# Expert routing rewritten as one selection pass with one place code, rounded-type counting matmuls, and a first expert pair that starts on its own gathered rows

## The reference, cut to what matters

```python
def hier_moe(h, w_group, b_group, w_expert, b_expert, w_gate, w_up, w_down):
    xt = h.reshape(-1, D); N = xt.shape[0]                       # 512 tokens
    g_prob = softmax(xt @ w_group + b_group)                      # 4 groups
    g_p, g_idx = lax.top_k(g_prob, 1)
    e_logits = (xt @ w_expert + b_expert).reshape(N, 4, 8)[the chosen group]
    e_p, e_idx = lax.top_k(softmax(e_logits), 2)
    w = g_p * e_p / sum(e_p)
    eid = g_idx * 8 + e_idx                                       # 2 of 32 experts per token
    # the rows of each expert are gathered into blocks, and each block does
    ys = (silu(xb @ w_gate[e]) * (xb @ w_up[e])) @ w_down[e]      # 1024 -> 256 -> 1024
    # out[token] = sum over its two experts of w * ys
```

## Time and profile before

| | us |
|---|---|
| median of 3 runs (1796.85 to 1800.13) | 1796.89 |
| the profiled execution | 1796.5 |
| its span in the profile | 1795.2 |
| TensorE busy | 1650.0 (92%) |
| VectorE busy | 938.2 (52%) |

### The profile page before, as it was taken

The page is one execution under the profiler, slowest core; times in us unless marked ns, Lnnn a source line. Parts: engine busy times, 40 slices in busy tenths (PEclk is TensorE's granted clock), DMA queues, the critical chain, the costliest instruction groups (busy, mean ns, idle before and its releaser), DMA issues.

```text
span 1795.2 us, 23753 instructions
## 1 busy us (share of the span) xinstructions
PE 1650.0 (92%) x8980; PEld 1202.1 (67%) x8980; DVE 938.2 (52%) x1869; ACT 699.9 (39%) x1518; POOL 357.4 (20%) x353
## 2 busy tenths in 40 slices
PE   6999879978999999998999599999999959999992
PEld 5887559966888888877888366667888743334330
DVE  4742674445677666665434866653344762323224
ACT  4432752245333334464322577774334531112111
POOL 0000635001222220000000255550010122333330
PEclk9999899989999999999999699999999979999996
DMA  6221000042344443341310000006114349999964
GB/s 277 107 94 47 1 1 1 1 188 78 143 178 177 181 182 141 129 188 48 141 47 24 0 8 8 8 8 258 68 74 187 139 164 352 400 372 394 383 250 158
DMA packets 40224, 251.66 MB, mean 140 GB/s; under 512 B 17904, under 2 KB 18032, under 8 KB 23600
## 3 DMA queue, kind: packets, MB, share of 16 engines
q1 hardware_dynamic: 23120, 223.49, 31.9%
q10 hardware_dynamic: 3168, 15.07, 2.2%
q0 software_dynamic: 13824, 11.58, 2.0%
HBM read 293.99 MB, written 18.87 MB: 174 GB/s over the span
## 4 chain that ended last, share of the span: by engine, by line
PE 85%; DVE 7%; DMA 3%; ACT 3%; issue 1%; SPq 0%; POOL 0%; DVEq 0%; ACTq 0%; POOLq 0%
PE banks L2214 17%; PE banks L2216 16%; PE banks L2215 16%; PE banks L2667 8%; PE banks L2152 7%; PE banks L2683 4%; PE banks L2275 3%; PE banks L2297 2%; DMA plain<-in_moe_gu,arena 2%; PE banks L2452 1%; PE banks L2458 1%; PE banks L2546 1%; PE banks L2463 1%; DVE units L1204 1%; ACT arena L623 1%
## 5 line engine op out<-in xcount | busy, mean ns | idle before, releaser
L623 ACT ACTIVATE units<-arena 128x512 fp32r<-128x512 f32 (+2 forms) x416 | 250.8, 626 | 475.8 <-PE banks L2216 471.2
L1204 DVE TENSOR_TENSOR units<-arena,units 128x512 fp32r<-128x512 f32 x370 | 252.2, 705 | 281.3 <-ACT units L623 281.0
L2214 PE MATMUL banks<-hx,units 128*128 128x512 f32 x800 | 314.8, 393 | 3.5 <-DVE arena L1655 1.7
L2216 PE MATMUL banks<-hx,units 128*128 128x512 f32 x800 | 312.0, 390 | 0.0
L2215 PE MATMUL banks<-hx,units 128*128 128x512 f32 x800 | 311.8, 390 | 0.0
L2214 PEld LDWEIGHTS banks<-hx,units 128*128 128x128 f32 x800 | 150.7, 188 | 35.5 <-issue 4.8
L2216 PEld LDWEIGHTS banks<-hx,units 128*128 128x128 f32 x800 | 150.5, 188 | 31.6
L2215 PEld LDWEIGHTS banks<-hx,units 128*128 128x128 f32 x800 | 150.8, 189 | 30.6
L2152 PE MATMUL banks<-arena 128*128 128x128 f32 (+2 forms) x768 | 120.2, 291 | 48.9 <-ACT arena L623 13.8
L623 ACT ACTIVATE arena<-banks 128x512 f32<-128x512 f32 (+3 forms) x194 | 107.3, 568 | 143.9 <-PE banks L2152 72.9
L2214 PE MATMUL banks<-units 128*128 128x512 f32 x380 | 151.0, 397 | 8.4 <-DVE units L1204 8.4
...
## 6 DMA issues: line engine op xcount, KB each, us to landing
...
```

Source lines behind the costliest of these rows:

```text
L623: return func(dst, src, ACT.Copy, scale=scale)
L1204: tt(lo, src, hi.bitcast(F32), SUB).then_inc(*up("gemm_dve", "lo", c.part, u))
L2214: pe.matmul(bs[i], sh[:, q], mh, start=c.first and k == 0, stop=False)
L2216: return pe.matmul(bs[i], sl[:, q], mh, start=False, stop=c.last and k == c.kn - 1)
```

## The change

- **Selection.** The logits' columns are reordered (experts first, groups last) and padded to 5 segments of 8 for each of 4 token tiles, so one pass of `first_max` over 20 segments chooses the group and the best expert of every group; a second pass with the winners masked gives the second. The three `first_max` become two, on 160 instead of 16 or 32 values. The fold and the running sums are gone. Padding and two small tables are written during `w_out21`.
- **Counting.** `mks`, triangle and ones are held in the rounded type (float32r). The running sums are made by more matmuls: 8 instead of 3. GpSimd copies the constants during `w_out21`.
- **Places.** Block and slot are one number, 64 times the block plus the slot; it is taken apart once after the selection.
- **Lists.** The one-hot tables are float32r; the list is read straight from PSUM in two operations instead of four.
- **Weights of the mix.** The five small operations stand after `idh`.
- **First pair.** GpSimd gathers block 0, then the overflow block, then starts the overflow weights, then gathers block 1. TensorE transposes block 0 only, runs the static `gate_up` of pair 0, and transposes the overflow block behind it.

```diff
         upper.close()
+        upper = ExitStack()
+        self.upper(upper, "front", [128, 1024], F32)
+        self.triR, self.onesR, self.ones64R = (self.upper(upper, "counts", [128, 128], F32R)[:, :] for _ in range(3))
+        self.mks, self.ohb = self.upper(upper, "picks", [128, 4, 32], F32R)[:, :, :], self.upper(upper, "lists", [128, 8, 2 * NBLK], F32R)[:, :, :]
+        self.ohi = self.upper(upper, "slots", [128, 2, 4, 128], F32R)[:, :, :, :]
+        upper.close()
...
-        self.lg, self.wr_c = self.new(4, 36), self.new(36)
+        self.lg, self.wr_c = self.new(4, 40), self.new(36)
+        self.e64, self.c31 = self.new(32), self.new(32)
+        assert self.top <= self.o_att + 9104
...
+        if k == 0:
+            v.memset(m.lg[:, :, 36:40], NEG)
+            ts(m.e64, K["iota32"], 64.0, None, MUL)
+            ts(m.c31, K["iota32"], -64.0, 1984.0, MUL, ADD).then_inc(*up("rx_dve", "tables"))
...
-    lg, go, ge, el, oh = m.lg, m.go, m.ge, m.el, m.oh
-
-    def first_max(vals, n, mx, onehot, tmp_):
-
-        io = bc(K["iota16"][:, 0:n].unsqueeze(1), 4, n)
-        ch(v.tensor_reduce(mx, vals, AX, ALU.max))
-        ch(tt(onehot, vals, bc(mx.unsqueeze(2), 4, n), ALU.is_equal))
-        ch(stt(tmp_, onehot, -64.0, io, MUL, ADD))
-        ch(v.tensor_reduce(R(15), tmp_, AX, ALU.min))
-        ch(tt(onehot, tmp_, bc(R(15).unsqueeze(2), 4, n), ALU.is_equal))
-
-    first_max(lg[:, :, 0:4], 4, R(0), go, ge)
-    ch(tt(ge, lg[:, :, 0:4], bc(R(0).unsqueeze(2), 4, 4), SUB), "gsub")
-    t3 = m.eg.rearrange("p t (g e) -> p t g e", g=4)
-    ch(tt(t3, lg[:, :, 4:36].rearrange("p t (g e) -> p t g e", g=4), bc(go.unsqueeze(3), 4, 4, 8), MUL))
-    ch(v.tensor_reduce(el, t3.rearrange("p t g e -> p t e g"), AX, ADD))
-    first_max(el, 8, R(2), oh[0], m.mk)
-    ch(stt(el, oh[0], NEG, el, MUL, ADD))
-    first_max(el, 8, R(3), oh[1], m.mk)
+    segs = m.lg.rearrange("p t (s e) -> p (t s) e", e=8)
+    by_seg = lambda ap: ap.rearrange("p (t s) -> p t s", t=4)
+    io = bc(K["iota16"][:, 0:8].unsqueeze(1), 20, 8)
+    mk2, q_ = m.mk2, m.q_
+    go = m.oh[0].rearrange("p (t s) e -> p t s e", t=4)[:, :, 4, 0:4]
+    for k in range(2):
+
+        onehot, mx = m.oh[k], m.mx[:, k, :]
+        ch(v.tensor_reduce(mx, segs, AX, ALU.max))
+        ch(tt(onehot, segs, bc(mx.unsqueeze(2), 20, 8), ALU.is_equal))
+        ch(stt(m.mk, onehot, -64.0, io, MUL, ADD))
+        ch(v.tensor_reduce(m.mn, m.mk, AX, ALU.min))
+        ch(tt(onehot, m.mk, bc(m.mn.unsqueeze(2), 20, 8), ALU.is_equal))
+        ch(tt(mk2[:, k].rearrange("p t (g e) -> p t g e", g=4),
+              onehot.rearrange("p (t s) e -> p t s e", t=4)[:, :, 0:4, :], bc(go.unsqueeze(3), 4, 4, 8), MUL))
+        if k == 0:
+            ch(tt(m.ge, m.lg[:, :, 32:36], bc(by_seg(mx)[:, :, 4].unsqueeze(2), 4, 4), SUB), "gsub")
+            ch(stt(segs, onehot, NEG, segs, MUL, ADD))
+    ch(tt(fl2(m.mks), fl2(mk2[:, 0]), fl2(mk2[:, 1]), ADD), "mks")
+    ch(tt(m.sel, m.mx.rearrange("p k (t s) -> p k t s", t=4)[:, :, :, 0:4], bc(go.unsqueeze(1), 2, 4, 4), MUL))
+    ch(v.tensor_reduce(m.rt[:, 2:4, :], m.sel, AX, ADD))
     ch(tt(R(4), R(3), R(2), SUB), "esub")
-    mk2, mks, q_, bp = m.mk2, m.mks, m.q_, m.bp
-    nov, cum, ob, hk = m.nov, m.cum, m.ob, m.hk
-    blk, pos = bp[:, 0], bp[:, 1]
-    bk, ik = m.bi[:, 0:8].rearrange("p (k t) -> p k t", k=2), m.bi[:, 8:16].rearrange("p (k t) -> p k t", k=2)
-    for k in range(2):
-        ch(tt(mk2[:, k].rearrange("p t (g e) -> p t g e", g=4), bc(go.unsqueeze(3), 4, 4, 8),
-              bc(oh[k].unsqueeze(2), 4, 4, 8), MUL))
-    ch(tt(mks[:, 0, :], fl2(mk2[:, 0]), fl2(mk2[:, 1]), ADD), "mks")
-    for t in range(1, 4):
-        ch(tt(mks[:, t, 0:32], mks[:, t - 1, 0:32], mks[:, 0, 32 * t:32 * t + 32], ADD), "sums", t)
-
-    v.wait_ge(*at("route_act", "gexp"))
-    ch(v.reduce_sum(R(1), ge, AX))
-    ch(v.reciprocal(R(1), R(1)))
-    v.wait_ge(*at("route_act", "eexp"))
-    ch(ts(R(5), R(4), 1.0, None, ADD))
-    ch(v.reciprocal(R(5), R(5)))
-    ch(tt(R(5), R(5), R(1), MUL))
+    nov, cum, ob = m.nov, m.cum, m.ob
     b = s.bank("route", "pos")
     places = b[:, 0:128].rearrange("p (t n) -> p t n", t=4)
     v.wait_ge(*at("route_pe", "pos"))
-    ch(ts(nov, b[:, 128:160], 1.0 / 64, -32.5 / 64, MUL, ADD))
+    ch(ts(nov, b[:, 128:160], -32.5 / 64, 0.0, ADD, ALU.max))
     ch(ts(nov, nov, RND, RND, ADD, SUB))
-    ch(ts(nov, nov, 0.0, None, ALU.max))
     ch(v.tensor_tensor_scan(cum, m.ones[:, 0:32], nov, 0.0, MUL, ADD))
     ch(tt(ob, cum, nov, SUB))
-    io32 = K["iota32"]
-    ch(stt(nov, ob, 31.0, io32, ADD, SUB))
-    ch(ts(q_, places, 1.0 / 64, -31.5 / 64, MUL, ADD))
-    ch(ts(q_, q_, RND, RND, ADD, SUB))
-    ch(stt(pos, q_, -64.0, places, MUL, ADD), "cnt")
-    ch(tt(blk, q_, bc(nov.unsqueeze(1), 4, 32), ADD))
-    ch(stt(blk, q_, 0.0, blk, ALU.is_gt, MUL))
-    ch(tt(blk, blk, bc(io32.unsqueeze(1), 4, 32), ADD))
-    ch(tt(m.both, bc(bp.rearrange("p a t n -> p a (t n)").unsqueeze(2), 2, 2, 128),
-          bc(mk2.rearrange("p k t n -> p k (t n)").unsqueeze(1), 2, 2, 128), MUL))
-    ch(v.tensor_reduce(m.bi, m.both.rearrange("p a k (t n) -> p (a k t) n", t=4), AX, ADD))
-    ch(ts(hk, bk, 0.5, -0.25, MUL, ADD))
-    ch(ts(hk, hk, RND, RND, ADD, SUB))
-    ch(stt(bk, hk, -2.0, bk, MUL, ADD))
-    ch(stt(ik, bk, 64.0, ik, MUL, ADD))
-    ch(tt(m.ohe, bc(K["iota"][:, 0:NBLK].unsqueeze(1), 8, NBLK),
-          bc(hk.rearrange("p k t -> p (k t)").unsqueeze(2), 8, NBLK), ALU.is_equal))
+    ch(stt(m.dlt, ob, 64.0, m.c31, MUL, ADD))
+    ch(tt(m.p0, places, bc(m.e64.unsqueeze(1), 4, 32), ADD))
+    ch(stt(q_, places, 63.5, bc(m.dlt.unsqueeze(1), 4, 32), ALU.is_gt, MUL), "cnt")
+    ch(tt(q_, q_, m.p0, ADD))
+    ch(tt(m.picked, bc(fl2(q_).unsqueeze(1), 2, 128), mk2.rearrange("p k t n -> p k (t n)"), MUL))
+    ch(v.tensor_reduce(m.code, m.picked.rearrange("p k (t n) -> p (k t) n", t=4), AX, ADD))
+    ch(ts(m.hk, m.code, 1.0 / 128, -127.0 / 256, MUL, ADD))
+    ch(ts(m.hk, m.hk, RND, RND, ADD, SUB))
+    ch(stt(m.ik.rearrange("p k t -> p (k t)"), m.hk, -128.0, m.code, MUL, ADD), "ik")
+    ch(tt(m.ohe, bc(K["iota"][:, 0:NBLK].unsqueeze(1), 8, NBLK), bc(m.hk.unsqueeze(2), 8, NBLK), ALU.is_equal))
     for n in range(2):
         ch(tt(m.ohb[:, :, NBLK * n:NBLK * n + NBLK], m.ohe, bc(K["tokv"][:, n, :].unsqueeze(2), 8, NBLK), MUL))
     for k in range(2):
-        ch(tt(m.ohi[:, k], bc(K["iota"].unsqueeze(1), 4, 128), bc(ik[:, k, :].unsqueeze(2), 4, 128), ALU.is_equal), "ohi", k)
-    tb_, td_, dd, ej, full = m.tb_, m.td_, m.dd, m.ej, m.full
+        ch(tt(m.ohi[:, k], bc(K["iota"].unsqueeze(1), 4, 128), bc(m.ik[:, k, :].unsqueeze(2), 4, 128), ALU.is_equal), "ohi", k)
+    io32 = K["iota32"]
+    td_, dd, ej, full = m.td_, m.dd, m.ej, m.full
     jj = bc(K["iota16"][:, 0:NDYN].unsqueeze(2), NDYN, 32)
     ch(tt(dd[:, 0], bc(ob.unsqueeze(1), NDYN, 32), jj, ALU.is_le))
     ch(tt(dd[:, 1], bc(cum.unsqueeze(1), NDYN, 32), jj, ALU.is_gt))
     ch(tt(dd[:, 0], dd[:, 0], dd[:, 1], MUL))
     ch(v.tensor_reduce(full, dd[:, 0], AX, ADD))
     v.wait_ge(*at("route_pe", "tok"))
-    ch(v.tensor_copy(fl2(tb_), s.bank("route", "tok")[:, 0:2 * NBLK]), "tb")
-    ch(ts(td_, tb_, 0.0, SKIP, ALU.is_equal, MUL))
-    ch(stt(td_, tb_, -1.0, td_, ADD, ADD))
-    ch(v.tensor_copy(m.idx, td_), "idx")
+    lists = s.bank("route", "tok")[:, 0:2 * NBLK]
+    ch(ts(fl2(td_), lists, 0.0, SKIP, ALU.is_equal, MUL))
+    ch(stt(fl2(m.idx), lists, -1.0, fl2(td_), ADD, ADD), "idx")
     ch(ts(full, full, -64.0, 64.0, MUL, ADD))
     ch(tt(dd[:, 0], dd[:, 0], bc(io32.unsqueeze(1), NDYN, 32), MUL))
     ch(v.tensor_reduce(ej, dd[:, 0], AX, ADD))
     ch(ts(m.idh[:, 0, :], ej, 2.0, None, MUL))
     ch(ts(m.idh[:, 1, :], ej, 2.0, 1.0, MUL, ADD), "idh")
+    v.wait_ge(*at("route_act", "gexp"))
+    ch(v.reduce_sum(R(1), m.ge, AX))
+    ch(v.reciprocal(R(1), R(1)))
+    v.wait_ge(*at("route_act", "eexp"))
+    ch(ts(R(5), R(4), 1.0, None, ADD))
+    ch(v.reciprocal(R(5), R(5)))
+    ch(tt(R(5), R(5), R(1), MUL))
...
     g.wait_ge(*at("gemm_pe", "step", "w_out21", 7))
+    g.tensor_copy(m.triR, K["triS"])
+    g.tensor_copy(m.onesR, m.ones)
+    ts(m.ones64R, m.ones, 1.0 / 64, None, MUL).then_inc(*up("moe_pool", "consts"))
     for ap in (*m.gx, m.gxd):
         ins = g.memset(ap, 0.0)
...
-    for i in range(2):
-        gather(m.gx[i], i, f"gx{i}", i)
+    gather(m.gx[0], 0, "gx0", 0)
     gather(m.gxd, NPAIR, "gxd", 0)
     g.wait_ge(*at("route", "idh"))
     g.wait_ge(*at("row_pe", "g2", 1))
     halves(0)
+    gather(m.gx[1], 1, "gx1", 1)
     downs(0)
...
     pe.wait_ge(*at("route", "mks"))
-    pe.matmul(b[:, 0:128], K["triS"], m.mks[:, 0, :], start=True, stop=False)
-    pe.wait_ge(*at("route", "sums", 3))
-    pe.matmul(b[:, 32:128].rearrange("p (t n) -> p t n", t=3), ones, m.mks[:, 0:3, 0:32], start=False, stop=False)
-    pe.matmul(b[:, 128:160], ones, m.mks[:, 3, 0:32], start=False, stop=True).then_inc(*up("route_pe", "pos"))
```

(15 more changed lines are left out.)

32 lines of the change are left out of this document (17 added, 15 removed).

## The result

| | kernel before | changed kernel |
|---|---|---|
| median (17 runs each) | 1797.74 us | 1792.66 us |
| range of the runs | 1794.04 to 1809.65 | 1788.43 to 1796.83 |
| ratio (95% interval) | | 0.9968 (0.9956 to 0.998) |
| the profiled execution | 1796.5 us | 1790.6 us |
| its span | 1795.2 us | 1789.3 us |

The change makes the kernel 5.8 us faster (3.6 to 7.9); the forecast was 5.6. The loop is as it was, TensorE busy for 69.25 of 70 us where the earlier trace rows have 69.33. The changed code lies ahead of it, and I go through it in the order of the prediction.

The account below looks back on a forecast made before the run. TensorE bounds the loop, which moves with its start, and that hangs on routing. Routing -3.3, gather +0.3 and first pair +3.2 give +0.2; with the hole's -5.8, -5.6 us: 1791.3 us, range 1787.5 to 1798.

Parts of the forecast that it names:

- Selection: Routing, VectorE's path to `mks`: 5.16 us against 5.66, a term of -0.5 us.
- places: Routing, VectorE from 1454.99 to the first half of L1972: 5.58 us against 7.44, a term of -1.9 us.
- lists: Routing: shorter list matmuls mostly covered, only a 0.23 us wait goes; two operations to `idx`; -0.2 and -0.4 us.
- Counting: Routing, from `mks` to the counts' first use: 1.6 us against 1.88; -0.3 us, between -1.0 and +0.2.
- The 3 small operations in `w_out21` and GpSimd's copies stand beside a busy TensorE: nothing, up to 0.3: Ahead of routing, during `w_out21`: the added small operations and copies cost nothing, up to 0.3 us.
- The gather: Behind the row numbers: the earlier gather meets the tail of SP's `down` weights, +0.3 of a possible 1.3 us.
- The first pair: Pair 0: +3.2 us from earlier static `gate_up` (-0.8), clock (+1.4), open overflow transposes with ScalarE's work (+2.6).
- The hole: Before pair 1's overflow `gate_up`: wait 0.4 us instead of 3.15, no half clock behind it; -5.8 us.
- Rival 2: Pair 1's fetch lands 12.6 us after its own issue, wait and half clock stay; 1797.1 us, no change; 14%.
- rivals 3 and 4: First pair: clock lost in the middle, 1794.7 us, 10%; the same loss with the hole kept, 1800.5 us, 9%.
- The sum: Whole kernel: +0.2 us to pair 0's overflow `gate_up` end, -5.8 for the hole; -5.6, giving 1791.3 us.
- a sign of being wrong: Beyond pair 1: any piece moving by other than the shift of the start would show the prediction wrong.

Follow-up runs that it names:

- e4: Changed kernel with the one-hot tables of the lists in f32 again; ratio to the kernel before 0.9959, median 1791.11 us.
- e3: Changed kernel with the three rounded constants made by ScalarE instead of GpSimd; ratio to the kernel before 0.9963, median 1791.57 us.
- e1: Changed kernel with the first pair and gather order of the kernel before, so routing alone; ratio to the kernel before 0.9978, median 1794.84 us.
- e5: Changed kernel with SP's static loads for pair 2 held until pair 0's overflow `gate_up` is done; ratio to the kernel before 1.0012, median 1800.57 us.
- e6: e3 with row numbers taken out of PSUM after two of the four overflow-table operations; ratio to the kernel before 0.9963, median 1792.26 us.
- e2: Kernel before with only the new first pair and order of gathers; ratio to the kernel before 0.999, median 1795.64 us.
- e7: e6 with the overflow block's transposes in the middle of pair 0's static `gate_up`; ratio to the kernel before 0.9994, median 1795.65 us.
- e8: e7 with SP holding pair 2's static weights until pair 1's overflow fetch has landed; ratio to the kernel before 1.0031, median 1804.57 us.
- e9: e8 without the split: overflow transposes again between pair 0's two `gate_up`; ratio to the kernel before 1.0046, median 1807.7 us.

## Why the prediction was right

**Selection, places, lists.** 5.15 us against 5.16 forecast, 5.58 against 5.58, and no wait for the list matmuls, as said. Interpolating the cost of a VectorE operation between two sizes of the same kind was good to 0.01 us an operation (0.36 for 160 values, 0.46 for 256). e4 shows that the shorter list matmuls were covered.

**Counting** was mis-sized, within its bounds: 2.04 us instead of 1.6, a loss of 0.2 where a gain of 0.3 was forecast. Eight rounded matmuls at half clock cost 0.23 us each (1.87 for the eight of the lists), as much as one pass of an f32 one in the earlier trace rows: rounding halves the number of passes, not their price, and five more matmuls ate what that gave. The clock had fallen at 1449.8 already, ahead of them, not in their midst as at 1453.4 before. In e3 the clock was still at 1.00 for the three of L2650, they stood 0.10 us apart (1454.16 to 1454.47), and counting took 1.40 us. The roughly 81 ns that the Trainium skill has for a matmul of 128 columns at full clock (TensorE: Matmul & The Clock Gate, section "Back-to-back issue gap") are near that, though these three have 32 to 96 columns; the changed kernel was not at full clock there.

**"The 3 small operations in `w_out21` and GpSimd's copies stand beside a busy TensorE: nothing, up to 0.3"** is the step that failed. It looked at TensorE for cover; the copies delayed GpSimd's memsets, and those hold back VectorE's L1177, which is on the path: 1.2 us in this profile. e3 shows it. In all eleven profiles the step ends 0.02 to 0.03 us after a memset does. With the copies on GpSimd it begins 1.28 to 1.29 us after the first memset, inside the second of three, in each of four profiles; in two of them (changed, e1) it was held until the third had ended, 1.47 us, and in two (e4, e5) only until the second had, 0.58. The changed kernel and e5 do not differ in this stretch, so no edit decides which of the two an execution gets, and the copies cost 0.3 or 1.2 us. Even the 0.27 of the kernel before is such a wait for the end of the last memset: the same kind of operation with no memset beside it, L1186, took 0.17. The Trainium skill (SBUF — State Buffer, section "SBUF: two separate sides") has a port pair that GpSimd and VectorE share and lock for a whole instruction; the trace agrees, as the step ends 0.02 us behind the memset, 1446.19 and 1446.17. With these two terms the row numbers came 1.7 us earlier, counted from the step, not 3.3, and outside the 2.8 to 4.0 that were given for them.

**The gather** took 4.67 us from the row numbers, 0.05 more than before instead of 0.3: the earlier it comes, the more it collides, and it came 1.1 us later than forecast (1465.03 for 1463.9). e6 measured the collision: all of a further 1.46 us.

**The first pair** cost +3.6 us, forecast +3.2: start of the `gate_up` at 3.77 instead of 3.6; clock 1.92 us lost instead of 2.0; transposes and pause 2.84 instead of 2.6.

**The hole** went as forecast: the fetch lands with SP's 4 MB (18.1 us behind them before and after), and both kernels that separate the two (e2, e5) agree. The wait was 0.14 us, forecast 0.4. e5 bears out that the fetch shares the DMA engines with what is queued ahead: the same fetch, 9.61 us with 4 MB far ahead and 14.95 with them close ahead. The Trainium skill (DMA: Bandwidth & Descriptors, section "Queues, rings and completion order") has each engine take turns between its queues packet by packet. The traces agree: where SP's and GpSimd's queues both had work, from 1494 to 1498 us, they moved 79 and 88 packets in the kernel before, 80 and 81 in e5, 76 and 79 in e7. With nothing of SP's ahead (e8) the fetch took at most 4.9. Rival 2 is thereby excluded; rivals 3 and 4 did not occur, as no pause of 1.75 us lowered the clock in any of these profiles.

**The sum.** Counted from the step, the end of pair 1's overflow `gate_up` came 4.0 us earlier (63.41 us before, 59.46 now); the forecast had 5.6. The miss is the one in routing, 1.6; those of the gather, the first pair and the hole (0.3, 0.4 and 0.1 us) nearly cancel. The other 1.9 us between the two profiles, whose spans differ by 5.9, belong to no term: 0.5 lie ahead of the step, and 1.5 came in the loop. There the kernel before has three waits of 0.4 to 0.9 us ahead of an overflow `gate_up`, two of them for a fetch, and the changed one a single one of 0.75. The prediction names this as a sign of being wrong, a piece beyond pair 1 that moves by other than the shift of the start. It is rather chance than an effect: from that point to the end, the profiles of the kernel before and of e1 to e7 have 286.1 to 287.4 us (286.6 in the kernel before), and the changed kernel has 285.1, the lowest. So the mechanism was right, and that the total of the profiles (5.9) meets the forecast (5.6) is in part luck; the interval of the runs, 3.6 to 7.9, holds 4.0 as well.

The rows also give a shorter account than the prediction's terms. TensorE takes up pair 1's overflow `gate_up` 18.2 to 18.5 us after SP's issue in every profile but e5, e8 and e9, and SP's issue hangs on the end of pair 0's static `gate_up`. That issue came 1.0 us earlier after the step than before (38.67 and 37.64 us), and so did the restart; the other 2.9 of the 4.0 us are the half clock that is gone. In e2 the restart is even 0.8 us later, and the kernel gains 2.2 by the clock alone. No run kept the clock up by any other means, so what that alone would bring without the new order is not shown.
